# Moving the small SBUF buffers of a two-block kernel in front of the split weights

## The reference, cut to what matters

```python
# first block, two layers
shift, scale, gate = jnp.split(jax.nn.silu(c) @ w_mod + b_mod, 3, axis=-1)
hx = _rmsnorm(x, norm_w) * (1 + scale[:, None]) + shift[:, None]
a_h, a_b, a_c, a_z, q, k, v, r_z = _split_in(hx @ w_in)          # 2048 x 8192
...
x = x + gate[:, None] * (jnp.concatenate([y_conv, y_ret], axis=-1) @ w_out)
# second block, one layer
proj = h @ w_in[i]                                               # 2048 x 6144
...
x = x + rms_norm(o @ w_out[i], ln_mix_post[i])
g, u = jnp.split(h @ w_gate_up[i], 2, axis=-1)                   # 2048 x 11264
f = (jax.nn.silu(g) * u) @ w_down[i]                             # 5632 x 2048
gate = jax.nn.sigmoid(rms_norm(x, ln_pli[i]) @ w_pli_gate[i])
x = x + gate * (p[i] @ w_pli_proj[i])
```

## The kernel before

| buffer | before | modulo 512 | changed | modulo 512 |
|---|---|---|---|---|
| X | 16512 | 128 | 16512 | 128 |
| raw | 49280 | 128 | 49280 | 128 |
| w_hi | 65664 | 128 | 67168 | 96 |
| w_lo | 82048 | 128 | 83552 | 96 |
| mats | 98432 | 128 | 99936 | 96 |
| cols, the first small one | 99456 | 128 | 65664 | 128 |
| act_hi, quarters, h_hi | 100960 | 96 | 100960 | 96 |
| act_lo | 133728 | 96 | 133728 | 96 |
| h_lo | 117344 | 96 | 117344 | 96 |
| f_hi | 138848 | 96 | 138848 | 96 |
| f_lo | 183904 | 96 | 183904 | 96 |
| a_raw | 166496 | 96 | 166496 | 96 |
| a_hi | 174688 | 96 | 174688 | 96 |
| a_lo | 182880 | 96 | 182880 | 96 |

## Time and profile before

### The profile page before, as it was taken

How to read it: one execution, slowest core, us unless ns; L and a number is a source line. 1 busy time by engine, 2 the same in 40 slices (tenths; PEclk the granted TensorE clock), 3 DMA queues, 4 the chain that set the end, 5 groups by cost and what they waited for, 6 DMA issues and landing times.

```text
span 2968.4 us, 45132 instructions
## 1 busy us (share of the span) xinstructions
PE 2913.9 (98%) x16565; PEld 2545.5 (86%) x16565; DVE 1827.9 (62%) x2354; ACT 1346.8 (45%) x1875; POOL 119.6 (4%) x129
## 2 busy tenths in 40 slices
PE   7899999999999999999999999999999999999999
PEld 4678887788888889998888899998999999988877
DVE  6868788878775346654446666665655555544464
ACT  6732222343443235444445577675544444434353
POOL 0000000010110000000011100000000000000000
PEclk9999999999999999999999999999999999999999
DMA  7855555444554226543334655555455555565554
GB/s 282 296 195 187 182 184 183 156 154 167 182 205 171 97 89 201 183 148 110 110 114 139 182 164 171 163 161 191 157 184 184 184 185 181 189 201 189 187 176 161
DMA packets 144750, 515.28 MB, mean 174 GB/s; under 512 B 16753, under 2 KB 16793, under 8 KB 142721
## 3 DMA queue, kind: packets, MB, share of 16 engines
q1 hardware_dynamic: 141264, 495.01, 50.6%
q0 software_dynamic: 3376, 18.77, 1.8%
HBM read 511.49 MB, written 2.22 MB: 173 GB/s over the span
## 4 chain that ended last, share of the span: by engine, by line
PE 91%; DVE 3%; ACT 2%; issue 2%; DMA 2%; DVEq 0%; ACTq 0%; POOL 0%; SPq 0%
PE main L1824 52%; PE main L1817 33%; PE aux L1776 2%; DVE w_lo L1104 1%; DMA raw<-in_w_mod 1%; PE aux L1977 1%; PE aux L1968 1%; ACT w_hi L626 1%; PE aux L2044 0%; PE aux L2028 0%; PE main L2192 0%; PE aux L2081 0%; PE aux L1980 0%; ACT u L934 0%; PE aux L1971 0%
## 5 line engine op out<-in xcount | busy, mean ns | idle before, releaser
L1104 DVE TENSOR_TENSOR w_lo<-raw,w_hi 128x1024 fp32r<-128x1024 f32 (+1 forms) x836 | 1012.3, 1212 | 859.0 <-ACT w_hi L626 850.1
L626 ACT ACTIVATE w_hi<-raw 128x1024 fp32r<-128x1024 f32 (+1 forms) x836 | 858.9, 1031 | 1267.3 <-PE main L1824 728.1
L1824 PE MATMUL main<-w_hi,act_hi 128*128 128x512 f32 (+1 forms) x1408 | 535.9, 381 | 2.9 <-DVE scores L1328 1.5
L1824 PE MATMUL main<-w_lo,act_hi 128*128 128x512 f32 (+1 forms) x1408 | 526.7, 374 | 0.0
L1824 PE MATMUL main<-w_hi,act_lo 128*128 128x512 f32 (+1 forms) x1408 | 526.7, 374 | 0.0
L1817 PE MATMUL main<-h_hi,w_hi 128*128 128x256 f32 x1408 | 395.9, 281 | 1.1 <-DVE h_lo L1250 1.1
L1817 PE MATMUL main<-h_hi,w_lo 128*128 128x256 f32 x1408 | 395.6, 281 | 0.0
L1817 PE MATMUL main<-h_lo,w_hi 128*128 128x256 f32 x1408 | 395.6, 281 | 0.0
L1824 PE MATMUL main<-w_hi,quarters 128*128 128x384 f32 (+1 forms) x1280 | 360.0, 353 | 0.0
L1817 PE MATMUL main<-act_hi,w_hi 128*128 128x256 f32 (+1 forms) x960 | 322.4, 336 | 2.4 <-DVE act_lo L1207 1.4
L1817 PE MATMUL main<-act_hi,w_lo 128*128 128x256 f32 (+1 forms) x960 | 321.0, 334 | 0.0
(11 more groups left out here) (307 smaller groups left out, 3296.5 us busy)
## 6 DMA issues: line engine op xcount, KB each, us to landing
raw<-in_w_ffn_up SPq DMA_DIRECT2D x176, 512.0 KB, 3.8
gates<-in_w_side SPq DMA_DIRECT2D x128, 512.0 KB, 3.5
raw<-in_w_in_ret SPq DMA_DIRECT2D x128, 512.0 KB, 4.1
raw<-in_w_in_conv SPq DMA_DIRECT2D x120, 512.0 KB, 4.1
raw<-in_w_out SPq DMA_DIRECT2D x96, 512.0 KB, 3.5
raw<-in_w_ffn_down SPq DMA_DIRECT2D x88, 512.0 KB, 3.6
raw<-in_w_mod SPq DMA_DIRECT2D x64, 512.0 KB, 4.6
raw<-in_w_sb SPq DMA_DIRECT2D x64, 384.0 KB, 3.3
```

The source lines that it names most:

```text
L626: A(w_hi[:, slot, 0:w], raw[:, slot, 0:w], ACT.Copy).then_inc(hi_split, 1)
L1104: V.tensor_tensor(out=w_lo[:, slot, 0:w], in0=raw[:, slot, 0:w], in1=w_hi[:, slot, 0:w].bitcast(F32), op=ALU.subtract).then_inc(lo_split, 1)
L1824: ins = mm(bank[:, c0:c1], x, w_part[:, slot, j * n + c0:j * n + c1], start=(k == 0 and j == 0 and i == 0), stop=(k == per - 1 and j == 1 ...
```

## The change

The nine small buffers (cols, ssq, rstd, rstd_root, table, scale_h, mix_a, ssq_fin, sum_fin; 1504 bytes with their rounding) are declared ahead of w_hi, w_lo and mats instead of behind them. So w_hi, w_lo and mats begin 1504 bytes later, the small ones 33792 bytes earlier, and all else stays where it was. 1504 is two times 512 and 480, so w_hi and w_lo go from 128 to 96 modulo 512, which is where all activation buffers of the main products begin. No instruction is added, removed or moved on any engine: the rows of all five engines are the same in the same order, 8498 on TensorE, 1143 on VectorE, 837 on ScalarE, 66 on GpSimd and 284 on SyncE. Only addresses differ.

```diff
         X = sb(top, "X", [P, 4 * D])
         raw = sb(top, "raw", [P, SLOTS, 1024])
-        w_hi = sb(top, "w_hi", [P, SLOTS, 1024], F32R)
-        w_lo = sb(top, "w_lo", [P, SLOTS, 1024], F32R)
-        mats = sb(top, "mats", [P, len(MATS) * P])
         cols = sb(top, "cols", [P, NCOLS])
         ssq = sb(top, "ssq", [P, 4, 4])
         rstd = sb(top, "rstd", [P, 4])
         rstd_root = sb(top, "rstd_root", [P, 4])
         table = sb(top, "table", [P, 1])
         scale_h = sb(top, "scale_h", [P, 4])
-
-        layer = ExitStack()
         mix_a = sb(top, "mix_a", [P, KT])
         ssq_fin = sb(top, "ssq_fin", [P, 2, 4])
         sum_fin = sb(top, "sum_fin", [P, 8])[:, 0:2]
+        w_hi = sb(top, "w_hi", [P, SLOTS, 1024], F32R)
+        w_lo = sb(top, "w_lo", [P, SLOTS, 1024], F32R)
+        mats = sb(top, "mats", [P, len(MATS) * P])
+
+        layer = ExitStack()
         act_hi = sb(layer, "act_hi", [P, KT * 512], F32R)
```

## The result

| | before | changed |
|---|---|---|
| median | 2971.43 us (2969.5 to 2972.63, 4 runs) | 2945.68 us (2944.55 to 2946.19, 4 runs) |
| ratio to before | | 0.9915, 95% interval 0.9903 to 0.9926 |
| profiled execution, span | 2970.15, 2968.4 us | 2945.76, 2944.0 us |
| VectorE, ScalarE busy | 1827.9, 1346.8 us | 1828.1, 1345.9 us |

The change makes the kernel 0.85% faster, 26 us. Forecast were 81 us and a range that ended at 2940.

The account below looks back on a forecast made before the run. TensorE was taken as the bound from 170 us on, by matmul count times distance between starts. Savings of 44.5 + 32.6 + 8.9 less 5 gave 81 us, so 2972 - 81 = 2891 us, range 2872 to 2940.

Parts of the forecast that it names:

- rival of no effect: Main products: a_bank's 226.7 ns comes from its buffers lying in another part of SBUF; time stays 2972 us; chance 0.12.
- Term 1: Main products of 512 columns, 6672 matmuls: each saves 6.67 ns, together 44.5 us.
- Term 2: Main products of 256 columns in ffn_up, in1_conv and in1_ret, 6528 matmuls: each saves 5.0 ns, together 32.6 us.
- two readings: At 256 columns the saving goes with the width, 3.3 ns, or belongs to the weight load, 6.67 ns; middle taken.
- Term 3: Matmuls of 384 columns, 1536 of them: each saves 5.8 ns, together 8.9 us.
- Term 4: Some 180 breaks of the main products by heads: 24 ns lost at each while the rhythm settles, 5 us taken.
- cover of the heads: Head chains through VectorE and ScalarE lose 3% of the TensorE work that covers them; costed at nothing.
- Terms 5 and 6: Splits on VectorE and ScalarE, and transposes by mats with small columns at new addresses: nothing added, cost nothing.
- mod0: The stretch up to 170 us waits for DMA and splits: no change.
- Narrow ones gain nothing: Weight loads back to back bind at 256 columns: 2924 us, or 2932 with 384 columns idle too; chance 0.12.
- half given back: Half the saving is lost to longer settling after breaks or to late heads: 2905 to 2920 us; chance 0.08.
- slower rival: At equal places each stream of 256 columns could meet its load; 10 ns more each gives 3008 us; chance 0.08.

Follow-up runs that it names:

- the map: Measuring kernel without the computation: blocks of 72 fp32r matmuls per width and r (stationary minus moving operand place, bytes); 226.7 ns at 512 columns, 119.9 at 256, r = 0.
- the nine kernels: Profiled executions of nine kernels that differ in addresses alone; the stretch up to the first matmul of L1817 lay between 168.9 and 172.6 us.

## Why the prediction was wrong, point by point

**The bound and the mechanism (right).** TensorE's starts set the time from 170 us on, and the distance between them follows the place of the operands: the run with the activations moved instead shows it without the weights' move. The Trainium skill, "TensorE: Matmul & The Clock Gate", section "Part 2: What happens when you issue a matmul", has two independent read ports and by it no effect at all; the trace and the map do not agree, with 226.7 to 237.3 ns at one shape. The rival of no effect, at 0.12, fell with it. That the period was 512 bytes was not needed for the sum; it is 256. The evidence against this rival leaned on the earlier trace rows, which hold no quarters at 512 columns; the trace before has such a run, at 72.82 / 312 = 233.4 ns, so the reading was right.

**Term 1, 512 columns (right in the rate).** 6.67 ns as forecast. In stages without stops between the pieces it came out whole: in0_conv 8.6 of 9.0 us, ffn_down 7.1 of 7.0, gate 2.5 of 2.6.

**Term 2, 256 columns (wrong in sign; this is the step that failed).** Forecast: -5.0 ns each, 32.6 us. Measured: +1.67 ns in ffn_up, +7.1 us, and +2.2 us in in1_conv. In in1_ret the timeline has the starts of each half. Before and changed, 12 matmuls of 256 columns, and in the changed kernel the 12 of 512 columns behind them:

```profile
1383.19 0.28 PE L1824 MATMUL main<-w_hi,act_hi 128*128 128x256 f32 x1
...
1384.59 0.40 PE L1824 MATMUL main<-w_hi,act_hi 128*128 128x512 f32 x1
```

```profile
1377.19 0.28 PE L1824 MATMUL main<-w_hi,act_hi 128*128 128x256 f32 x1
...
1378.62 0.40 PE L1824 MATMUL main<-w_hi,act_hi 128*128 128x512 f32 x1
...
1381.37 0.28 PE L1824 MATMUL main<-w_hi,act_hi 128*128 128x256 f32 x1
```

1.40 us for 12 is 116.7 ns, 1.43 is 119.2 (it settles at 120.0): over the 768 such matmuls 2.0 us lost. The 12 of 512 columns take 2.75 us, 229.2 ns each, since the first five distances behind the change of width are still 228 to 236 ns. Together some 11 us lost at 256 columns where 33 were to be won, 44 of the 55 us that are missing. My two readings both took the 6.67 ns saved at 512 columns as a clash that the change removes and asked only how it scales. But at equal places TensorE still pays 13.3 ns for each matmul, and in the old place it paid 20.0 ns at 512 columns and 11.7 (weights stationary) or 10.0 (weights moving) at 256: the cost of the old place depended on the width, that of the new one does not. Zero as the lower bound was the mistake behind it. The row to take seriously was the difference already in hand, 118.3 - 106.7 = 11.7 ns, smaller than the 226.7 - 213.3 = 13.3 ns of `a_bank`. Had I carried `a_bank`'s extra over as a constant per matmul, I would have had 120.0 and 173.3 ns. The trace before also had 118.3 and 116.7 ns at 256 columns for the two roles, a sign that counts, which the prediction read as one value that fits. That a constant is the truer reading was not to be seen from one width, but it was as good a guess as the two that I took.

**Term 3, 384 columns (wrong in size).** Forecast: 8.9 us. Added up over all distances between starts at 384 columns, 261.7 us became 261.1: 0.6 us gained. The run of 12 with 174 ns, from which the term started, was no measure of what the placement costs. In the kernel before, of the 68 runs of such matmuls 49 end at 173.3 ns, which is 384 / 2.4 + 13.3 already, and 19 at about 176.7. One of each kind, 9 matmuls in 1.59 us and 6 in 1.04:

```profile
1746.46 0.34 PE L1824 MATMUL main<-w_lo,quarters 128*128 128x384 f32 x1
...
1748.05 0.34 PE L1824 MATMUL main<-w_lo,quarters 128*128 128x384 f32 x1
...
1753.86 0.34 PE L1824 MATMUL main<-w_lo,quarters 128*128 128x384 f32 x1
...
1754.90 0.34 PE L1824 MATMUL main<-w_lo,quarters 128*128 128x384 f32 x1
```

In the changed kernel 66 of the 68 end at 173.3 ns, but many have single distances of 176 to 185 ns before they settle, so that little is left. The 384 matmuls of 512 columns in sb, dil and out2 gave 2.3 us.

**Term 4, restarts (about right), and the cover of the heads (costed at nothing, 2 us).** in0_ret and out0 got 12.3 of 15.4 us. Of the 3.1 us, 2.0 are a wait that grew: L1968 for VectorE's kT, which stands behind the side pieces of L1167 in VectorE's queue (at 754.4 to 757.5 us in the chain of the changed kernel, for one). The waits of TensorE, before and changed:

```profile
PE aux L1968 <- DVE kT L1374: 0.8, 1, 0.8
```

```profile
PE aux L1968 <- DVE kT L1374: 2.8, 6, 1.2
```

The rest, 1 us, is left for restarts in that stretch. In in1_ret and out1 the distances of 512 columns gave 5.5 of 7.7 us, so 2.2 us went to settling after heads and changes of width; the prediction had named the heads alone.

**Terms 5 and 6, the splits, mod0 (right).** 1249 and 1058 ns as before. Only the reason given in term 6 and in the bound of term 2 does not stand on the earlier trace rows: fp32r matmuls of 128 columns have 111.7 ns too in the map, so 111 ns for fp32 products of that width doesn't tell two column times for each column from a bound of the load. The 3.0 us at the start lie within the scatter of the nine kernels.

**The rivals.** Narrow ones gain nothing (2924 to 2932) was nearest; half given back had a size too small and a wrong cause. The mechanism of the slower rival was half right: at one place modulo 256 a matmul of 256 columns does cost more, but 1.67 ns in ffn_up and some 2.5 in in1_ret, and not the 5.5 ns from which it would have decided.

**Open.** Why r = 0 costs 13.3 ns at three widths, why the pattern over r and over the place within 32 bytes is as it is, and what picks one of two rhythms, no run here tells; the maps describe it and don't explain it. In all 64 runs of in1_ret at 256 columns with r = 0 the changed kernel settled at 120.0 ns; whether a distance of 0 always has one rhythm only is not shown. 113.3 ns at r = 52 and 88 was not tried in the whole kernel: it needs weights off the multiples of 32 bytes in ffn_up alone. r = 64, which had the same value in 44 runs of in1_ret, was not tried with ffn_up. in1_conv with a distance of its own was not tried either, since in1_ret uses the same activations the other way round.

## What to carry to other kernels

Where fp32r matmuls with a load each stand end to end, divide a long run of the chain by its count for every shape, and compare it with width / 2.4: what is above is worth a trial of placements, one per shape, since the best place for 512 columns cost time at 256. Read short runs from the starts in the timeline, each width by itself, and several of them: at 384 columns a single run of 12 stood for two rhythms. A kernel that only runs such matmuls over all distances takes 0.7 ms and showed the real kernel's values to 0.2 ns in the long runs of ffn_up and ffn_down, as long as both kept their operands on multiples of 32 bytes. For short runs between other work it can be off by 3 to 5 ns (384 columns at r = -32, 256 at r = 64). A natural experiment within the trace proves its own shape only: bound another width on both sides of zero unless a row of that width stands there.

## What the runs showed of the hardware that I had not expected

- The distance between starts of fp32r matmuls depends on where the two operands lie against each other modulo 256 bytes, in the maps between 226.7 and 237.3 ns at 512 columns and between 113.3 and 122.2 ns at 256 with the moving operand on a multiple of 32 bytes, and with the sign: r = -64 and 64 gave 229.0 and 233.3 ns at 512 columns.
- One shape in one placement can run in two rhythms, each pair within one execution: 173.3 or 176.7 ns at 384 columns with r = -32, 113.3 or 117.8 at 256 columns with r = 64, and in the map, with nothing changed but what ran before, 116.7 or 117.8 at 256 columns with r = -32.
- The place within 32 bytes that both share counts too: with r = 0, 226.7 ns on a multiple of 32 bytes and 237.8 ns 4 bytes past one, at 512 columns.
- A matmul of 128 columns takes 111.7 ns in a run with a load each, at all nine distances of the map (the first block's 111.0 comes from its start; its last rhythm is 111.7).
